# Each dense product of 512 moving columns issued as two of 256 columns with the same stationary tile

## The reference

```python
p = hn @ w_in[l]                                   # 1024 x 6912: RWKV and retention projections, gates
merged = sigmoid(g_rw) * (y_rw @ w_branch_rw[l]) + sigmoid(g_ret) * (y_ret @ w_branch_ret[l])
h = h + rms_norm(merged @ w_out[l], norm_mix_post[l])
f = (gelu(gate) * val) @ w_down                    # after u = h @ w_up, 1024 x 5632, and a short convolution
# second block
zxbcdt = u @ in_w                                  # Mamba-2 layer, 1024 x 5152
y.astype(h.dtype) @ out_w                          # 2048 x 1024
q, gate = jnp.split(u @ in_w, 2, axis=-1)          # attention layer, 1024 x 2048; also kv_w
(o * jax.nn.silu(gate)) @ out_w
g = sigmoid(rms_norm_2(h, norm_w) @ gate_w); g * (p_i @ proj_w)    # twice
```

## Time and profile before

| | |
|---|---|
| time, median of 3 runs | 944.76 us (944.45 to 944.95) |
| span of the profiled execution, first to last instruction | 943.0 us |
| PE busy | 909.9 us (96%), 5705 matmuls |
| weight loads busy | 799.4 us (85%), 5705 |
| DVE busy | 685.4 us (73%) |
| ACT busy | 513.4 us (54%) |
| mean granted clock of TensorE | 0.993 |
| DMA | 136.63 MB, mean 145 GB/s |

### The profile page before, as it was taken

How to read it: one execution, slowest core, us unless ns; L and a number is a source line. 1 busy time by engine, 2 the same in 40 slices (tenths; PEclk the granted TensorE clock), 3 DMA queues, 4 the chain that set the end, 5 groups by cost and what they waited for, 6 DMA issues and landing times.

```text
span 943.0 us, 14451 instructions
## 1 busy us (share of the span) xinstructions
PE 909.9 (96%) x5705; PEld 799.4 (85%) x5705; DVE 685.4 (73%) x970; ACT 513.4 (54%) x734; POOL 96.6 (10%) x91
## 2 busy tenths in 40 slices
PE   6999999999999989999999899999999998999998
PEld 6998998988888769999988689988878786878777
DVE  6688836783878678888863667787687687776665
ACT  6863332233555366656643655766475667477543
POOL 6002421430000000000000000006320000000000
PEclk9999999999999999999999999999999999999999
DMA  9543132212465364665655544643223453632231
GB/s 307 169 148 107 59 107 62 84 46 90 159 220 178 135 220 138 201 201 179 200 201 180 178 135 140 201 160 131 90 91 129 151 178 131 205 123 90 90 110 69
DMA packets 80979, 136.63 MB, mean 145 GB/s; under 512 B 3957, under 2 KB 46545, under 8 KB 80912
## 3 DMA queue, kind: packets, MB, share of 16 engines
q1 hardware_dynamic: 78800, 131.17, 42.1%
q0 software_dynamic: 2112, 4.53, 1.5%
HBM read 134.64 MB, written 1.05 MB: 144 GB/s over the span
## 4 chain that ended last, share of the span: by engine, by line
PE 63%; DVE 6%; ACT 5%; issue 3%; DMA 1%; DVEq 0%; ACTq 0%
PE bank L437 18%; PE bank L439 17%; PE bank L438 17%; PE bank L426 3%; DVE lower L1861 2%; ACT upper L1297 2%; PE bank L1076 1%; PE bank L881 1%; PE bank L889 1%; PE bank L1060 1%; DVE arena L2401 1%; ACT arena L1777 1%; PE bank L684 1%; DMA loaded<-in_ffn_w_up 1%; DMA loaded<-in_ple_gate_w 1%
## 5 line engine op out<-in xcount | busy, mean ns | idle before, releaser
L1861 DVE TENSOR_TENSOR lower<-loaded,upper 128x2048 fp32r<-128x2048 f32 x122 | 279.7, 2296 | 123.6 <-ACT upper L1297 121.5
L1297 ACT ACTIVATE upper<-loaded 128x2048 fp32r<-128x2048 f32 x122 | 231.9, 1903 | 115.3 <-PE bank L439 101.5
L437 PE MATMUL bank<-xT_upper,upper 128*128 128x256 f32 (+1 forms) x664 | 187.4, 282 | 2.0 <-DVE xT_lower L1926 1.8
L438 PE MATMUL bank<-xT_lower,upper 128*128 128x256 f32 (+1 forms) x664 | 185.7, 280 | 0.0
L439 PE MATMUL bank<-xT_upper,lower 128*128 128x256 f32 (+1 forms) x664 | 185.6, 280 | 0.0
L437 PE MATMUL bank<-upper,xT_upper 128*128 128x512 f32 (+1 forms) x360 | 146.2, 406 | 4.7 <-DVE lower L1861 3.5
L439 PE MATMUL bank<-upper,xT_lower 128*128 128x512 f32 (+1 forms) x360 | 139.8, 388 | 0.0
L438 PE MATMUL bank<-lower,xT_upper 128*128 128x512 f32 (+1 forms) x360 | 139.3, 387 | 0.0
L437 PEld LDWEIGHTS bank<-xT_upper,upper 128*128 128x128 f32 (+1 forms) x664 | 125.8, 190 | 3.3 <-issue 2.7
L438 PEld LDWEIGHTS bank<-xT_lower,upper 128*128 128x128 f32 (+1 forms) x664 | 125.9, 190 | 0.1
L439 PEld LDWEIGHTS bank<-xT_upper,lower 128*128 128x128 f32 (+1 forms) x664 | 125.9, 190 | 0.1
(11 more groups left out here) (340 smaller groups left out, 1209.4 us busy)
## 6 DMA issues: line engine op xcount, KB each, us to landing
loaded<-in_w_in SPq DMA_DIRECT2D x26, 1024.0 KB, 5.1
loaded<-in_ffn_w_up SPq DMA_DIRECT2D x22, 1024.0 KB, 5.1
loaded<-in_ssm_in_w SPq DMA_DIRECT2D x20, 1024.0 KB, 5.3
loaded<-in_ffn_w_down SPq DMA_DIRECT2D x11, 1024.0 KB, 5.0
loaded<-in_ssm_out_w SPq DMA_DIRECT2D x8, 1024.0 KB, 5.0
loaded<-in_ple_gate_w SPq DMA_DIRECT2D x8, 1024.0 KB, 5.1
loaded<-in_attn_in_w SPq DMA_DIRECT2D x8, 1024.0 KB, 5.2
loaded<-in_w_branch_ret SPq DMA_DIRECT2D x4, 1024.0 KB, 5.0
```

The lines of the kernel that those rows point to most:

```text
L437: mm(out, a[0], b[0], start=start, stop=False)
L438: mm(out, a[0], b[1], start=False, stop=False)
L1297: A(part(upper, PARTS, n), part(loaded, LOADS, n), ACT.Copy).then_inc(uppers, 1)
L1861: TT(part(lower, LOADS, n), part(loaded, LOADS, n), part(upper, PARTS, n).bitcast(F32), sub) \
```

## The change

Where the output is 512 columns wide, `mm3` issues six matmuls in place of three. Each goes to one half of the same bank, takes one half of the moving tile, and has the same stationary tile as its neighbour. The first half of the first product carries the start flag, the second half of the last product the stop flag. Outputs under 512 columns are made as before. Nothing else is changed: the order of the products, the semaphores and what the other engines do stay.

```diff
             def mm3(out, a, b, start, stop):

-                mm(out, a[0], b[0], start=start, stop=False)
-                mm(out, a[0], b[1], start=False, stop=False)
-                return mm(out, a[1], b[0], start=False, stop=stop)
+                if out.shape[-1] < 512:
+                    mm(out, a[0], b[0], start=start, stop=False)
+                    mm(out, a[0], b[1], start=False, stop=False)
+                    return mm(out, a[1], b[0], start=False, stop=stop)
+                c, d = slice(0, 256), slice(256, 512)
+                mm(out[:, c], a[0], b[0][:, c], start=start, stop=False)
+                mm(out[:, d], a[0], b[0][:, d], start=False, stop=False)
+                mm(out[:, c], a[0], b[1][:, c], start=False, stop=False)
+                mm(out[:, d], a[0], b[1][:, d], start=False, stop=False)
+                mm(out[:, c], a[1], b[0][:, c], start=False, stop=False)
+                return mm(out[:, d], a[1], b[0][:, d], start=False, stop=stop)
```

## The result

The changed kernel takes 951.66 us (median of 4 runs, 948.24 to 952.51) against 944.61 us for the kernel before (943.67 to 944.95): a ratio of 1.0068 with a 95% interval of 1.0048 to 1.0087, 7 us slower. The forecast was 3 us faster, and the range ended at 951.0. The profiled execution has a span of 950.7 us, 7.7 us more than before.

What follows compares the result with a forecast made beforehand. PE, busy 910 of 943 us, was taken as the bound. The split products' -8.3 us plus 0.27 x 17.2 gave -3.7, 9 tenths of it -3.3: 944.8 - 3.3 = 941.5 us, range 936.5 to 951.0.

Steps and rivals of the forecast that it cites:

- The step that failed: Dense PE stretches: each was taken to draw 113.3 or 117.8 ns per 256-column matmul after small products, whatever its operands.
- -8.3 + 0.27 x 17.2: Sum for the 1920 split products: all at 113.3 ns gives -8.3 us; 27% at 117.8 ns makes it -3.7 us.
- the higher level: The slower pitch of 256-column matmuls on PE, 117.8 ns against 113.3; 27% of the turned products had it.
- The nearest row: Hand-cut last product, `xT` stationary, 256 columns: 17 starts 113.1 ns apart, taken to speak for the faster pitch with `xT`.
- the bounds for the two levels: All split products at 113.3 ns would give -8.3 us, all at 117.8 ns +8.9 us.
- 9 tenths: Share of a PE gain let through to the kernel's time, as PE has 909.9 of 943.0 us: -3.7 becomes -3.3 us.
- The slower rival: Weight loads without slack set the pitch of split products, mostly 117.8 ns: up to +8.9 us, 952.8 us; chance 0.18.
- "The level follows the operands": Split products: arena pairs cost 235.6 ns, those with `xT` 226.6, together -0.4 us, 944.4 us; chance 0.18.
- The fixed price for each matmul: Each of 1920 added matmuls on PE costs 2.3 ns, +4.4 us, 948.8 us; chance 0.07.
- Zeros that held: Side effects of the split priced at zero: repeated stationary tile, alternating bank halves, waits at starts, added instructions, other engines.
- the repeated tile: Neighbouring matmuls with the same stationary tile: 379 ns each against 378 with different tiles, so no price taken.
- instruction fetch: Instruction queues: 1920 more matmuls with loads move some 0.25 MB more than 0.92 MB, at zero cost.

Runs made afterwards that it cites:

- the split kernel at distance 64: Changed kernel with tiles moved so each dense class has its stationary tile 64 bytes from its moving one, modulo 256: 946.48 us, ratio 1.0027.
- the whole kernel at distance 0: Kernel before, unsplit, with `xT` and most arena tiles moved to 0 bytes from the weights modulo 256, turned products at 64: 940.47 us, ratio 0.9961.

## Why the prediction was wrong

- **The step that failed** is "I see no operand, bank or unit slot that separates them: each new stretch after small products seems to draw its level", and the sum made from it, -8.3 + 0.27 x 17.2. I took the 27% of the turned products for the split ones. But the roles are exchanged: there the weight is stationary and `xT` moves, here the other way, so the distance has the other sign, 192 in place of 64. At 192 the higher level held 95% of the places, and in the sum -8.3 + share x 17.2 the share would have to be 92%, not 27, to give the 7.5 us measured by pitch. The turned products went to 117.6 ns too where a placement put them at 192. In eight placements whole classes moved with their distance, and at distance 64 the split products were cheaper than the whole ones, at 0 they cost 19 us more; that is shown. Within distance 64 the level does change with the unchanged code (the up projection at 113.3 and 117.8 ns), so the change of level that I saw is real; its share isn't a constant that carries over.
- **The nearest row** The earlier trace rows had the right operands and columns and was still an exception: 17 rows of one stretch, at the same distance 192. The last product of the changed kernel, with the last matmul ahead of it, first and last of 22 rows:

```profile
944.11 0.28 PE L447 MATMUL bank<-upper,xT_lower 128*128 128x256 f32 x1
...
946.58 0.28 PE L440 MATMUL bank<-upper,xT_lower 128*128 128x256 f32 x1
```

  2.47 us / 21 = 117.6 ns between starts. A stretch of 17 is one draw, not 17.
- **The counts, the bounds for the two levels and the unit prices** were right: with both classes at the higher level the text had +8.9 us; measured +7.5 by pitch. That there are two levels only was not: the arena had 116.7 ns in the down projection and 118.3 to 118.6 in the products before it. All of it came through, not 9 tenths: 7.7 us of span.
- **The slower rival** had the number nearly right (952.8 us, from the higher level for nearly all) and the mechanism wrong: short loads left the pitch at 117.3 ns. So that its number came near is luck.
- **"The level follows the operands"** was right in kind and wrong in the sign for `xT`: it had the arena at 117.8 and `xT` at 113.3. The arena's 4.4 ns over `xT` with 512 columns are one of distance too: at 192 the arena's whole products take 229.0 ns as well.
- **The fixed price for each matmul**: a pair costs less than the whole at distance 64 (226.6 against 233.3 ns in the long stretches; 232.2 against 233.3 as the mean over all of `xT`) and 13.3 more at 0 (240.0 against 226.7). No constant price does that. By the rule of the Trainium skill ("TensorE: Matmul & The Clock Gate", "Back-to-back issue gap"), which the section gives for the isolated gap of single matmuls, the split costs some 2.5 ns a product wherever the tiles lie; the runs have -6.7 to +13.3, and none came to its 215.8 ns for 512 columns (the least is 226.7).
- **Zeros that held**: the repeated tile, the alternation of halves, the waits, instruction fetch (1.17 MB in place of 0.92, as forecast), the other engines: all that isn't dense matmuls took 266.2 us before and after.

Open: why the distance matters. That PE reads the two tiles at once and that these reads disturb one another fits the table, but no run shows the reads; nor why 256 and 512 columns prefer different distances, or what makes a stretch at distance 64 take one of its two levels. The 12 times of the split kernel at distance 64 lie in two groups, 945.2 to 946.6 and 948.5 to 950.9 us, which the up projection's 4.6 us would make if each execution drew anew; with one trace for each kernel that isn't shown. Other distances than those of the table, and different ones for the upper and lower parts, weren't tried. What the first matmul of a stretch costs by itself was not worked out either.

## What to carry to other kernels

A price read in one class of matmuls holds for the roles and addresses of its two operands: before it is used for another, compare where the stationary and the moving tile lie to each other, and count stretches, not rows. Splitting a matmul of 512 columns changed its price by -7 to +13 ns in the long stretches, by where the tiles lay, so try the placement with the form unchanged first: moving tensors and units by some bytes gave 4.5 us by median (ratio 0.9961) here. Where runs of one kernel spread by more than the effect, the pitch of the long stretches in the trace tells kernels apart that the times can't.

## What was not expected of the hardware

- The pitch of matmuls with the same code went from 113.3 to 120.0 ns (256 columns) and from 226.7 to 233.3 ns (512 columns) when tensors moved by 64 bytes, with a period of 256 bytes in the distances that were run.
- Nearly every stretch holds one level to the end: 1040 matmuls of the up projection at 113.3 ns in one kernel's trace and at 117.8 in another's, with the same instructions. In the whole kernel at distance 0 the turned stretch from 584.0 us began at 120.0 ns and went on at 113.3.
- Weight loads of 64 in place of 128 columns (0.13 in place of 0.19 us) beside 256 moving columns left the pitch of the long stretch nearly where it was (117.3 and 117.8 ns).
- 384 + 128 columns cost 286 ns, 256 + 256 cost 227 to 240.
